# First block of a two-block transformer kernel: rotary halves exchanged by a VectorE shuffle in place of a TensorE permutation, handled one step later; row maxima negated straight into the exponentials' bias, one wait per softmax component

## The reference, cut to what matters

```python
def rotate(x, cos, sin):
    x1, x2 = jnp.split(x, 2, axis=-1)
    return jnp.concatenate([x1 * cos - x2 * sin, x2 * cos + x1 * sin], axis=-1)

# differential attention: 4 heads, 2 components each, 64 wide; the first 16 of the 64 are rotated
q = jnp.concatenate([rotate(q[..., :ROPE_DIM], cos, sin), q[..., ROPE_DIM:]], axis=-1)
k = ...
q = q * (A_QK_DIM ** -0.5)
p = jax.nn.softmax(jnp.where(mask, sc, NEG_INF), axis=-1)      # per component c
w = p[:, :, 0] - lam * p[:, :, 1]
return jnp.einsum('bhqk,bhkv->bhqv', w, vh)

# retention: 4 heads, all 64 of q and k are rotated, halves of 32
q = rotate(q, cos, sin)
k = rotate(k, cos, sin) * (R_QK_DIM ** -0.5)
```

## Time and profile before

| | |
|---|---|
| median of 3 runs | 3851.65 us (3850.85 to 3853.29) |
| the profiled execution, its own time | 3852.72 us |
| its span, first to last instruction | 3850.9 us |
| busy, PE / PEld / DVE / ACT / POOL | 3701.6 / 2832.3 / 1759.4 / 1107.3 / 1408.3 us |
| mean granted TensorE clock | 0.988 |

### The profile page before, as it was taken

One profiled execution on the slowest core, in us unless ns is written; L12 is line 12 of the kernel. 1 busy time (PEld: TensorE's weight loads), 2 busy tenths in 40 slices (PEclk: granted clock), 3 DMA queues, 4 the chain that ended last, 5 costly groups with the idle time before them and its releaser, 6 DMA issues.

```text
span 3850.9 us, 43042 instructions
## 1 busy us (share of the span) xinstructions
PE 3701.6 (96%) x16664; PEld 2832.3 (74%) x16664; DVE 1759.4 (46%) x2125; ACT 1107.3 (29%) x1819; POOL 1408.3 (37%) x734
## 2 busy tenths in 40 slices
PE   6999999999999999999999999999899999999999
PEld 5666788887778666788887787777666678766667
DVE  4555113223145655204213235882566579345654
ACT  3334100112212333210102212123455331435542
POOL 2212344343356222244442347442323255333324
PEclk9999999999999999999999999999899999999999
DMA  4000111111124100111111114311111231111122
GB/s 151 28 27 28 47 53 46 49 47 33 39 88 142 33 28 28 44 51 48 47 52 33 33 44 139 104 39 33 37 29 31 80 122 50 33 32 33 34 70 90
DMA packets 74684, 209.40 MB, mean 54 GB/s; under 512 B 8224, under 2 KB 13600, under 8 KB 74016
## 3 DMA queue, kind: packets, MB, share of 16 engines
q1 hardware_dynamic: 53712, 159.15, 14.0%
q10 hardware_dynamic: 20816, 48.01, 3.5%
HBM read 186.16 MB, written 20.97 MB: 54 GB/s over the span
## 4 chain that ended last, share of the span: by engine, by line
PE 88%; DVE 8%; ACT 3%; issue 1%; DMA 0%; SPq 0%; ACTq 0%; DVEq 0%
PE psA L502 45%; PE psT L483 17%; PE psA L483 7%; PE psA L1819 3%; PE psA L728 2%; PE psT L1886 2%; PE psT L778 2%; PE psT L1790 1%; PE psT L1795 1%; DVE b_rowmax L1274 1%; PE psT L1863 1%; ACT X L992 1%; PE psT L1860 1%; PE psT L706 1%; PE psT L700 1%
## 5 line engine op out<-in xcount | busy, mean ns | idle before, releaser
L449 POOL TENSOR_TENSOR Whi<-stage,credit 128x1024 fp32r<-128x1024 f32 (+2 forms) x364 | 600.6, 1650 | 2394.8 <-PE psA L502 1200.0
L452 POOL TENSOR_TENSOR Wlo<-stage,Whi 128x1024 fp32r<-128x1024 f32 (+2 forms) x364 | 807.4, 2218 | 28.6
L502 PE MATMUL psA<-Hhi,Whi 128*128 128x512 f32 x2240 | 702.6, 395 | 0.4 <-DVE b_ypad L2327 0.4
L502 PE MATMUL psA<-Hlo,Whi 128*128 128x512 f32 x2240 | 690.2, 389 | 0.0
L502 PE MATMUL psA<-Hhi,Wlo 128*128 128x512 f32 x2240 | 689.9, 389 | 0.0
L502 PEld LDWEIGHTS psA<-Hhi,Whi 128*128 128x128 f32 x2240 | 419.2, 188 | 101.3 <-issue 16.6
L502 PEld LDWEIGHTS psA<-Hlo,Whi 128*128 128x128 f32 x2240 | 420.5, 188 | 88.1
L502 PEld LDWEIGHTS psA<-Hhi,Wlo 128*128 128x128 f32 x2240 | 420.5, 188 | 88.1
L483 PE MATMUL psT<-Hhi,Whi 128*128 128x512 f32 x1024 | 426.9, 417 | 33.1 <-ACT b_upad L1015 15.0
L483 PE MATMUL psT<-Hhi,Wlo 128*128 128x512 f32 x1024 | 406.5, 397 | 0.0
L483 PE MATMUL psT<-Hlo,Whi 128*128 128x512 f32 x1024 | 406.5, 397 | 0.0
(11 more groups left out here) (320 smaller groups left out, 4883.4 us busy)
## 6 DMA issues: line engine op xcount, KB each, us to landing
stage<-in_w SPq DMA_DIRECT2D x232, 512.0 KB, 3.5
stage<-in_w SPq DMA_DIRECT2D x68, 256.0 KB, 2.6
xs<-X ACTq DMA_DIRECT2D x8, 2048.0 KB, 8.0
stage<-in_w SPq DMA_DIRECT2D x32, 384.0 KB, 3.1
b_wk<-xs ACTq DMA_DIRECT2D x36, 256.0 KB, 5.2
rope<-in_ropes ACTq DMA_DIRECT2D x4, 1024.0 KB, 5.0
stage<-in_w SPq DMA_DIRECT2D x32, 128.0 KB, 2.1
X<-xs ACTq DMA_DIRECT2D x8, 512.0 KB, 8.1
```

The source lines that it names most:

```text
L449: pool.tensor_tensor(Whi[:, b, 0:n], stage[:, b, 0:n], credit[:, 0:1].broadcast_to([P, n]), ALU.add).then_inc(s.w_hi, 1)
L452: pool.tensor_tensor(Wlo[:, b, 0:n], stage[:, b, 0:n], Whi[:, b, 0:n].bitcast(F32), ALU.subtract).then_inc(s.w_split, 1)
L502: mm = pe.matmul(dst[h], w[:, cols], r[k][:, h * HALF:(h + 1) * HALF], start=first and k == order[0] and r is rhi and w is whi, stop=last ...
```

## The change

The pieces `sq` and `sk` and the retention's `swap` go away, with their constants. A rotary piece is now: VectorE waits for the projection in PSUM, shuffles it into ROT (each partition is exchanged with another one within its 32), multiplies the projection by cosine, which frees the bank, multiplies ROT by sine, and adds. The scale of the scores goes into the factors of q. ScalarE no longer copies q and k. In the attention's steps VectorE holds q and k pieces back in `late`, so they come behind the next step's `mix` and `maxima`. In retention rq and rk are read from psA the same way; their weight columns and rotary tables are ordered so that partners lie within 32 partitions. `maxima` reduces component 1 first, writes the negated maximum straight to the bias, and counts its semaphore once per component; `exps` and `mix` take component 1 first with a wait of its own. Two input tiles and lamraw share a buffer `first`, which is twice as large.

```diff
-B1_PRELUDE = [("q", 0, 0), ("k", 0, 0), ("sq", 0, 0), ("sk", 0, 0), ("q", 0, 1), ("k", 0, 1), ("sq", 0, 1),
-              ("sk", 0, 1), ("v", 0, 0), ("v", 0, 1)]
+B1_PRELUDE = [("q", 0, 0), ("k", 0, 0), ("q", 0, 1), ("k", 0, 1), ("v", 0, 0), ("v", 0, 1)]
...
-            ([("sq", 1, 0)], [("k", 1, 0), ("b0", 0, 0, True), ("ss", -1, 1)]),
-            ([], [("sq", 1, 1), ("k", 1, 1), ("b0", 0, 1, True)]),
-            ([("sk", 1, 0)], [("z", 0, 0)]),
-            ([("sk", 1, 1)], [("z", 0, 1)]),
+            ([], [("k", 1, 0), ("b0", 0, 0, True), ("ss", -1, 1)]),
+            ([], [("k", 1, 1), ("b0", 0, 1, True)]),
+            ([], [("z", 0, 0)]),
+            ([], [("z", 0, 1)]),
...
+def exchange(half):
+
+    return [i ^ half if i < 2 * half else i for i in range(32)]
...
-        nmax = Tally(sem("nmax"), HEADS * NT)
+        nmax = Tally(sem("nmax"), 2 * HEADS * NT)
...
                 if L == 0:
                     pe.wait_ge(setup, 1)
+                    pe.wait_ge(x_copied, NT)
                 scores(L, 0, 0)
...
-                pe.wait_ge(rtab_in, 48)
-                swap(L, ("swaprq", 0), ("rq", 0), swapr, R_RAWQ)
-                swap(L, ("swaprk", 0), ("rk", 0), swapr, R_RAWK)
...
             def exps(L, h, q):
-                act.wait_ge(*nmax.upto(L, h * NT + q + 1))
                 n = (q + 1) * P
-                for c in (0, 1):
+                for c in (1, 0):
                     use = ("s", h, q, c)
+                    act.wait_ge(*nmax.upto(L, 2 * (h * NT + q) + 2 - c))
                     act.activation(PR[q % 2][c][:, 0:n], psA[:, A.buf(use), 0:n], ACT.Exp,
-                                   bias=negmax[:, q % 2, c:c + 1], scale=SCALE,
+                                   bias=negmax[:, q % 2, c:c + 1],
                                    accum_out=rowsum[:, q % 2, c:c + 1]).then_inc(A.freed(use), 1)
...
-                if kind in ("q", "k", "v"):
+                if kind == "v":
                     act.wait_ge(*F.filled(L, use))
-                    dst = {"q": AQ[h % 2], "k": AK[h % 2], "v": RAW}[kind]
-                    act.activation(dst[:, c], psF, ACT.Copy).then_inc(F.freed(use), 1)
+                    act.activation(RAW[:, c], psF, ACT.Copy).then_inc(F.freed(use), 1)
...
+            def rotate(L, use, dst, done):
+
+                raw = psA[:, A.buf(use)]
+                dve.wait_ge(*A.filled(L, use))
+                if use[0] == "rk":
+                    dve.wait_ge(*r_rot.upto(L, 2 * use[1] + 1))
+                step(dve.stream_shuffle(R_ROT, raw, exchange(16)))
+                dve.tensor_tensor(dst, raw, rope[:, 0], ALU.mult).then_inc(A.freed(use), 1)
+                step(dve.tensor_tensor(R_ROT, R_ROT, rope[:, 1], ALU.mult))
+                dve.wait_ge(*A.drained(L, use))
                 dve.tensor_tensor(dst, dst, R_ROT, ALU.add).then_inc(done, 1)
 
             def maxima(L, h, q):
                 n = (q + 1) * P
-                for c in (0, 1):
+                for c in (1, 0):
                     use = ("s", h, q, c)
-                    dve.wait_ge(*A.filled(L, use))
-                    step(dve.reduce_max(rowmax[:, c:c + 1], psA[:, A.buf(use), 0:n], AX_X))
-                dve.tensor_scalar(negmax[:, q % 2], rowmax[:], -SCALE, None, ALU.mult).then_inc(nmax.sem, 1)
+                    dve.wait_ge(*A.filled(L, ("s", h, q, 1)))
+                    dve.reduce_max(negmax[:, q % 2, c:c + 1], psA[:, A.buf(use), 0:n], AX_X, negate=True)\
+                        .then_inc(nmax.sem, 1)
 
             def mix(L, h, q):
...
+                dve.wait_ge(*A.drained(L, ("s", h, q, 1)))
+                step(dve.reciprocal(inv[:, q % 2, 1:2], rowsum[:, q % 2, 1:2]))
+                step(dve.tensor_scalar(p1, p1, inv[:, q % 2, 1:2], lam[:, 4:5], ALU.mult, ALU.mult))
                 dve.wait_ge(*A.drained(L, ("s", h, q, 0)))
...
+                step(dve.reciprocal(inv[:, q % 2, 0:1], rowsum[:, q % 2, 0:1]))
                 dve.scalar_tensor_tensor(out=p0, in0=p0, scalar=inv[:, q % 2, 0:1], in1=p1, op0=ALU.mult, op1=ALU.add)\
                     .then_inc(mixed.sem, 1)
...
+                if kind in ("q", "k"):
+                    dst = (AQ if kind == "q" else AK)[h % 2][:, c]
                     dve.wait_ge(*F.filled(L, use))
...
+                    step(dve.stream_shuffle(ROT, psF, exchange(8)))
+                    scale = SCALE if kind == "q" else 1.0
+                    dve.scalar_tensor_tensor(out=dst, in0=psF, scalar=scale, in1=rope[:, 0, c], op0=ALU.mult,
+                                             op1=ALU.mult).then_inc(F.freed(use), 1)
+                    step(dve.scalar_tensor_tensor(out=ROT, in0=ROT, scalar=scale, in1=rope[:, 1, c], op0=ALU.mult,
+                                                  op1=ALU.mult))
                     dve.wait_ge(*F.drained(L, use))
                     dve.tensor_tensor(dst, dst, ROT, ALU.add).then_inc(rotated.sem, 1)
...
-                                if use[0] == "ss":
+                                if use[0] in ("ss", "q", "k"):
                                     late.append(use)
...
-                take(L, ("rq", 0), R_RAWQ)
-                take(L, ("rk", 0), R_RAWK)
```

More of the change, by code:

```diff
@@ L355 @@
     mask = 256
[L356 to L364, removed]
+    swapm = 384
+    causal = 512
+    dmask = 640
+    xi = 640 + 512
+    zeta = 640 + 768
+    decay = 640 + 1024
+    n = 640 + 1024 + 2
 def build(nc, x, w1, par1, lamv, finalg, w2, par2, pww, sgw, sgb, consts, ropes, ng, out, xs):
@@ L557, in first_block @@
         tok = sb("tok", [P, 2, NT])
-        first = sb("first", [P, SEQ])
+        first = sb("first", [P, 2, SEQ])
+        lamraw = first[:, 0, 0:DEPTH * 4 * A_QK].rearrange("p (l c) -> p l c", l=DEPTH)
         a_uses, t_uses = uses_of_block1()
@@ L576, in first_block @@
         summed, rstd, h_scaled, h_hi, h_lo = env.summed, env.rstd, env.h_scaled, env.h_hi, env.h_lo
-        consts_in, params_in, swapa_in, rtab_in = (sem(n) for n in ("consts_in", "params_in", "swapa_in", "rtab_in"))
+        consts_in, params_in, rtab_in = (sem(n) for n in ("consts_in", "params_in", "rtab_in"))
         x_in = [sem(f"x_in{t}") for t in range(NT)]
@@ L608, in first_block @@
         TMP, ROT = upad[:, 2:2 + HALF], upad[:, 2 + HALF:]
-        XT = [first[:], upad[:, 2:]] + [wk[:, t] for t in range(2, NT)]
+        XT = [first[:, 0], first[:, 1]] + [wk[:, t] for t in range(2, NT)]
         Y, JUNK = [rtab[:, 0:D_MODEL], rraw[:, 0]], psT[:, 1]
@@ L707, in turn @@
                 return mm
[L709 to L713, removed]
             def scores(L, h, q):
@@ L748, in piece @@
                     pe.wait_ge(s.w_split, L * NP + p + 3)
-                if kind in ("sq", "sk", "vt"):
-                    source = ({"sq": "q", "sk": "k", "vt": "v"}[kind], h, half)
+                if kind == "vt":
+                    source = ("v", h, half)
                     if F.buf(source) != F.buf(use):
@@ L760, in piece @@
                                          arrived if kind == "q" and h == 0 else None)
-                elif kind in ("sq", "sk"):
-                    mm = pe.matmul(psF, swapa[:], (AQ if kind == "sq" else AK)[h % 2][:, c], start=True, stop=True)
                 elif kind == "vt":
@@ L1258, in step @@
                 dve_step.step(dve, ins)
-            def rotate(L, use, raw, raw_tile, dst, done):
-                dve.wait_ge(*A.drained(L, raw))
-                step(dve.tensor_tensor(dst, raw_tile, rope[:, 0], ALU.mult))
-                dve.wait_ge(*T.filled(L, use))
-                dve.tensor_tensor(R_ROT, psT[:, T.buf(use)], rope[:, 1], ALU.mult).then_inc(T.freed(use), 1)
-                dve.wait_ge(*T.drained(L, use))
+            def rotate(L, use, dst, done):
[7 more added lines that the diff above has]
+                dve.wait_ge(*A.drained(L, use))
                 dve.tensor_tensor(dst, dst, R_ROT, ALU.add).then_inc(done, 1)
@@ L1290, in piece @@
                 c, psF = slice(half * HALF, (half + 1) * HALF), bank(use)
-                if kind in ("sq", "sk"):
-                    dst = (AQ if kind == "sq" else AK)[h % 2][:, c]
+                if kind in ("q", "k"):
+                    dst = (AQ if kind == "q" else AK)[h % 2][:, c]
                     dve.wait_ge(*F.filled(L, use))
-                    dve.tensor_tensor(ROT, psF, rope[:, 1, c], ALU.mult).then_inc(F.freed(use), 1)
-                    step(dve.tensor_tensor(dst, dst, rope[:, 0, c], ALU.mult))
+                    step(dve.stream_shuffle(ROT, psF, exchange(8)))
[4 more added lines that the diff above has]
+                                                  op1=ALU.mult))
                     dve.wait_ge(*F.drained(L, use))
                     dve.tensor_tensor(dst, dst, ROT, ALU.add).then_inc(rotated.sem, 1)
-                    dve.wait_ge(*rotated.upto(L, rotations(h, kind[1], half)))
+                    dve.wait_ge(*rotated.upto(L, rotations(h, kind, half)))
                 elif kind == "vt":
@@ L1344, in attention @@
```

(12 more changed lines are left out.)

38 lines of the change are left out of this document (12 added, 26 removed).

## The result

The changed kernel takes 3809.23 us (median of 4 runs, 3809.13 to 3812.24) against 3851.26 for the kernel before, measured beside it: a ratio of 0.9889, 95% interval 0.9877 to 0.9901, so 42.0 us or 1.1% less. The profiled execution's own time is 3809.13, its span 3807.3; the forecast was 3810.5.

A forecast was written before the change was run, and what follows sets the result against it. TensorE, busy in 96% of the span, was taken to bound the kernel; attention 21.8, prelude 7.5 and retention 11.9 make 41.2 us off 3852.7, 3811.5, lowered for the median to 3810.5; range 3800 to 3827.

The forecast's parts named there:

- Steps of the attention: All attention heads of both layers: 10.9 us gained a layer, 21.8 in all.
- Step 1: Attention heads 0 to 2: q's second half waits for its bank, 3.15 us behind the scores; loss 2.5.
- Steps 3 and 4: Attention heads 1 and 2: k's second half 3.7 us behind the scores, then the z half 3.97 behind.
- Step 5: Attention: next z half needs only its twin's bank; masks and transposes take 0.9 us; gain 2.5.
- The v half: Attention, steps 6 and 7: it starts 10.2 us behind the scores instead of 12.03; gain 1.8.
- Step 2 of head 0: Attention: no bank wait before k's second half, but VectorE is late beside GpSimd's split; gain 0.9 us.
- Prelude and start: Ahead of each layer's attention: eight matmuls fewer, 3.6 us a layer, less a 0.7 wait, plus 0.5 per start; 7.5 together.
- Retention: 16 permutation matmuls removed, 14.1 us, less waits of 1.1 for ScalarE's square, one a layer; gain 11.9.
- the clock: Rival: granted clock falls in the attention's new waits, sixteen places at 0.7 us make 11, 3822 us; chance 0.12.
- the overlap: Attention, before v and at layer starts: exponentials run during the second maximum; with L1275 lost, 1.8 us before v.
- The rival slower than before: VectorE as bank holder delays projections at 17 places, 2.9 us each beyond the 1.75 allowed: 3860 us; chance 0.03.

The follow-up runs named there:

- joint waits: Changed kernel with the negated maximum kept, but exponentials and mix waiting for both components, one reciprocal for the two: 3806.58 us, ratio 0.9878 to the kernel before.

## Why the prediction was right, point by point

The sum was 41.2; the medians differ by 42.0, the profiled executions by 43.6. Each term can be read between the same marks of the two chains.

- **Steps of the attention, 21.8 expected.** From the first scores(1) to the first panel of the merge, layer 0 took 326.3 us (90.22 to 416.48) and takes 315.7 (85.88 to 401.56): 10.6. Layer 1: 326.9 (1267.14 to 1594.08) against 314.1 (1241.59 to 1555.70): 12.8. Together 23.4.
- **Step 1, the new wait.** Expected behind the scores 3.15, measured 2.81. The shuffle was priced at 0.85 and takes 0.74, and two maxima without a wait between them take 0.96 where 1.12 was set. Right in place and kind.
- **Steps 3 and 4.** Expected 3.70 and 3.97, measured 3.33 and 3.62, for the same reason.
- **Step 5.** Expected 0.9, measured 0.87. **The v half.** Expected 10.2, measured 10.11.
- **Step 2 of head 0.** From the scores' end to the second half of k: 10.17 before (1283.97 to 1294.14), 8.98 now (1258.96 to 1267.94), 1.2 gained where 0.9 was expected. VectorE beside GpSimd's split holds it, 2.85 for the sine product at 1261.90.
- **Prelude and start, 7.5 expected.** Layer 0: scores(1) come 4.3 us earlier. Layer 1: 3.3, of which the prelude's wait of 0.7 is a part. Together 7.6.
- **Retention, 11.9 expected, 11.5 measured**, with two waits of 1.11 where 1.1 was given.
- **What is left over.** The three terms make 42.5 of the 43.6. Another 1.6 lies between retention and the prelude of layer 1, where the kernel before had a granted clock of 0.79 (1140 to 1148 us) and the changed one ran at full speed; what follows the retention of layer 1 gives 0.5 back. No term stood for either.
- **What was missed: the clock.** It was a rival at 0.12 and no term of the sum. At single pieces it is one: the second halves of q and k in head 1 take 7.3 us instead of 5.7, and the first q piece of layer 0 takes 7.10 where it had taken 6.16. In the total it comes to nothing, as the granted clock over the attentions is 0.99 and 0.98 before (40 to 420 and 1210 to 1600 us) and 0.98 and 0.99 after (40 to 410 and 1190 to 1560). These losses took the place of others, such as those before v (6.29 and 6.33 before, 5.72 now), which the range had given as a gain of up to 5. The bank waits came out 0.35 shorter at each of 16 places, 5.6 us, but the attention gained only 1.6 beyond the forecast; the 4 us between were not taken apart. The mechanism was right; that the total came within 1.3 us was in part luck, as a second set of runs of the same kernel has its median at 3806.51 and a profiled execution at 3799.17. The Trainium skill (TensorE: Matmul & The Clock Gate, section on HAM oscillation) has recurring idle gaps send TensorE back to half speed; the runs agree for the waits of steps 1 and 3, each with granted clock 0.79 around the piece behind it, and show that it is not certain: see below.
- **The reason for the new maxima.** I had put the gain before v down to the lost L1275 and the overlap together. The lost L1275 alone suffices (10.31 with joint waits); whether the overlap alone would is not shown.
- **The rival slower than before** needed 2.9 us more at each place. The run without holding back lost the gain in another way, 0.2% slower than before, by putting rotation and mix behind one another. The mechanism is the one named, VectorE as the holder of what TensorE needs next; the guard against it was the order of work, which I had not priced by itself: 49 us, of which 28 are waits by the two profiles and the rest goes with the clock.

## What to carry to other kernels

When work is moved from the engine that bounds a kernel to another one, its place in that engine's stream is worth as much as the work: the same four VectorE operations gave 3859, 3809 or 3770 us, behind their own step's pieces, behind the next maxima, or ahead of them. Look for the moment at which the helper waits for the bounding engine anyway, and put the operation that frees a buffer there. An overlap that costs nothing to give up in one order can be worth 14 us in another, about half of it in waits, so price such edits again once the waits have moved.

## What the runs showed of the hardware

A VectorE shuffle within 32 partitions from PSUM takes 0.74 us for 512 columns and 1.32 for 1024, and loading its pattern 14 ns. Copies from PSUM take 0.68 and 1.22, so the shuffle is dearer by 8% (1.13 ns a column between the two widths, the copy 1.05). All shuffles of the changed kernel in groups (busy, mean ns of one):

```profile
L1276 DVE STREAM_SHUFFLE b_upad<-psT 128x512 f32<-128x512 f32 x32 | 23.6, 738 | 0.0
L1244 DVE STREAM_SHUFFLE b_rraw<-psA 128x1024 f32<-128x1024 f32 x8 | 10.5, 1316 | 0.0
```

The same wait doesn't always cost the same. The changed kernel was profiled twice. Around the second half of q in head 1 of layer 1, which begins 2.8 us behind the scores in both, the stretches read (length; busy PE, PEld, DVE, ACT, POOL; granted clock; DMA share; GB/s), in the first profile and in the second:

```profile
1326.00:1334.00 8.00, 7.86 (x28) 5.86 (x28) 3.31 (x7) 0.00 (x0) 0.00 (x0) 0.79 0.00 0
```

```profile
1325.00:1332.00 7.00, 6.43 (x28) 4.73 (x28) 3.74 (x8) 0.13 (x1) 0.00 (x0) 1.00 0.00 0
```

The piece took 7.32 us in the one and 5.68 in the other. A wait of this length can send TensorE to its lower level of 1.2 GHz or leave it at 2.4, with the same instructions before it. Shorter ones can too: behind the 1.11 us wait in retention the granted clock fell in both layers of the run with retention alone, in one layer of the second profile of the changed kernel (0.79 from 2046 to 2054 us), and in none of the first. The two executions took 3809.13 and 3799.17 us. Of these 10 us the two attentions hold 4.7 (315.7 and 314.1 us against 312.6 and 312.5), and the rest lies outside them. A difference of a few us between two kernels says little until the granted clock of both is compared.

What GpSimd's split holds up depends on the operation beside it. The negation of two columns took up to 2.26 us, of one column never over 0.16, and the sum of two tiles in SBUF 2.77 instead of 0.69.
